# One-core hybrid attention layer: score bias and mask added on VectorE, gate units in another order, low halves on GpSimd

## The reference, cut to what matters

```python
mod = silu(c) @ w_ada + b_ada; shift, scale, gate = split(mod, 3)
h = rmsnorm(x, ln_gain) * (1 + scale) + shift
q_a, ckv, krope, g_a, q_b, k_b, v_b, q_i, k_i, w_i, g_b = split(h @ w_in)
# group A: latent attention, chunk-causal mask        -> o_a
# group B: an indexer scores keys, top-k keys per row are kept (k = 64 prompt, 36 sample), then
s = (q_b . k_sel) * 128**-0.5 + rel_bias[rel_bucket(sel - q_pos)]
s = where(valid, s, -inf);  o_b = softmax(s) @ v_sel
y = concat(rmsnorm(o_a, gain_a) * silu(g_a), rmsnorm(o_b, gain_b) * silu(g_b))
out = rmsnorm(x + gate * (y @ w_out), final_gain)
```

## Time and profile before

| what | value |
|---|---|
| time, 3 runs | median 1014.14 us (1013.35 to 1014.65) |
| profiled execution, own time | 1013.96 us |
| its span | 1012.2 us |
| TensorE busy | 941.5 us, 93% of the span, mean granted clock 0.986 |
| VectorE, ScalarE, GpSimd busy | 419.3, 341.0, 91.3 us |

### The profile page before, as it was taken

One profiled execution on the slowest core, in us unless ns is written; L12 is line 12 of the kernel. 1 busy time (PEld: TensorE's weight loads), 2 busy tenths in 40 slices (PEclk: granted clock), 3 DMA queues, 4 the chain that ended last, 5 costly groups with the idle time before them and its releaser, 6 DMA issues.

```text
span 1012.2 us, 14472 instructions
## 1 busy us (share of the span) xinstructions
PE 941.5 (93%) x5867; PEld 808.4 (80%) x5867; DVE 419.3 (41%) x865; ACT 341.0 (34%) x629; POOL 91.3 (9%) x165
## 2 busy tenths in 40 slices
PE   3798789999999999999999999999998899899996
PEld 0466577899998788888898998889986789688885
DVE  2222343436332244432324632349454346745562
ACT  2332342334212243323314522233333336433342
POOL 1000022102100000111102100010011001300000
PEclk9999899999999999999999999999999899899999
DMA  8999956665533224564426765345576536864423
GB/s 318 386 335 368 365 164 170 156 159 140 151 115 94 79 87 138 151 194 128 135 85 184 240 212 178 92 126 177 185 237 214 181 102 241 293 209 130 135 64 125
DMA packets 128403, 183.29 MB, mean 181 GB/s; under 512 B 29408, under 2 KB 79256, under 8 KB 127184
## 3 DMA queue, kind: packets, MB, share of 16 engines
q1 hardware_dynamic: 115744, 138.71, 44.1%
q0 software_dynamic: 12592, 43.65, 12.9%
HBM read 171.80 MB, written 10.52 MB: 180 GB/s over the span
## 4 chain that ended last, share of the span: by engine, by line
PE 84%; DMA 5%; ACT 3%; DVE 3%; issue 2%; SPq 2%; POOL 1%; DVEq 0%; ACTq 0%; POOLq 0%
PE proj L1697 31%; PE proj L1686 28%; PE proj L1713 2%; PE bankO L1670 2%; DMA araw<-in_w_ada 2%; SPq L696 2%; PE bankO L1794 1%; PE bankO L1803 1%; PE bankS L1713 1%; PE bankS L1686 1%; PE proj L1670 1%; PE bankS L1920 1%; PE bankT L1935 1%; DMA kload<-in_cache_dsa_k 1%; DMA raw<-in_w_in 1%
## 5 line engine op out<-in xcount | busy, mean ns | idle before, releaser
L1255 DVE TENSOR_TENSOR w_lo<-raw,w_hi 128x1024 fp32r<-128x1024 f32 (+2 forms) x164 | 193.6, 1185 | 233.2 <-ACT w_hi L919 232.8
L919 ACT ACTIVATE w_hi<-raw 128x1024 fp32r<-128x1024 f32 (+2 forms) x164 | 167.4, 1027 | 210.0 <-PE proj L1686 126.1
L1697 PE MATMUL proj<-hT_hi,w_hi 128*128 128x384 f32 x640 | 222.3, 347 | 1.1 <-ACT misc L919 1.1
L1697 PE MATMUL proj<-hT_hi,w_lo 128*128 128x384 f32 x640 | 214.8, 336 | 0.0
L1697 PE MATMUL proj<-hT_lo,w_hi 128*128 128x384 f32 x640 | 214.7, 335 | 0.0
L1686 PE MATMUL proj<-w_hi,hT_hi 128*128 128x512 f32 (+2 forms) x464 | 180.9, 390 | 16.1 <-DVE w_lo L1255 13.2
L1686 PE MATMUL proj<-w_lo,hT_hi 128*128 128x512 f32 (+2 forms) x464 | 176.6, 381 | 0.0
L1686 PE MATMUL proj<-w_hi,hT_lo 128*128 128x512 f32 (+2 forms) x464 | 176.5, 380 | 0.0
L1697 PEld LDWEIGHTS proj<-hT_hi,w_hi 128*128 128x128 f32 x640 | 120.7, 189 | 9.1 <-issue 7.0
L1697 PEld LDWEIGHTS proj<-hT_lo,w_hi 128*128 128x128 f32 x640 | 120.7, 189 | 0.7 <-issue 0.2
L1697 PEld LDWEIGHTS proj<-hT_hi,w_lo 128*128 128x128 f32 x640 | 120.5, 188 | 0.0
(11 more groups left out here) (346 smaller groups left out, 1033.3 us busy)
## 6 DMA issues: line engine op xcount, KB each, us to landing
raw<-in_w_in SPq DMA_DIRECT2D x104, 512.0 KB, 3.8
araw<-in_w_ada SPq DMA_DIRECT2D x128, 256.0 KB, 7.6
raw<-in_w_ada SPq DMA_DIRECT2D x32, 512.0 KB, 3.8
raw<-in_w_out SPq DMA_DIRECT2D x32, 512.0 KB, 3.9
raw<-in_w_in SPq DMA_DIRECT2D x32, 256.0 KB, 3.2
raw<-in_w_in SPq DMA_DIRECT2D x32, 128.0 KB, 2.5
wuk<-in_w_uk POOLq DMA_DIRECT2D x16, 256.0 KB, 3.7
kload<-in_cache_dsa_k POOLq DMA_DIRECT2D x8, 512.0 KB, 5.3
```

The lines of the kernel that those rows point to most:

```text
L919: return nc.scalar.activation(out, in_, func, scale=scale, **kw)
L1255: V.tensor_tensor(w_lo[:, SLOT[u], 0:w], raw_of(u)[:, 0:w], high(u)[:, 0:w].bitcast(F32), ALU.subtract).then_inc(lo_ready, 1)
L1697: ins = mm(banks[blk][:, 0:TOK], w[:, n, cols], a[:, kt, :], start=first and n == m == 0, stop=final and n == per - 1 and m == 2)
```

## The change

1. `units()` puts one `gate` unit behind each unit of `qi` and of `qb` (32 in all) and none elsewhere.
2. The matrices `rev` and `rep`, their loads and the matmuls with them are gone. The bias rows are written once to DRAM 128 times over (`skew_d`, 2 MB, from DRAM to DRAM at the place of the old bias read), so that a stride of one less than a row reads them in the order that the scores have. Prompt: VectorE adds mask and bias per head (`masked_bias`, for head h + 1 between the maximum and the wait for the exponential of head h). Sample: the mask goes to DRAM and comes back in eight DMAs into `comb` (`ld_mask`), VectorE adds the bias to it once (`comb`, 128 x 1152), and per sequence one operation adds `comb` to the scores and takes the maximum; a sign change follows, and ScalarE's exponential reads SBUF, where it read PSUM.
3. `yh`'s low half is on GpSimd, where it was on VectorE.
4. Group B's gate tiles have eight buffers of their own (`gl_b`); loads, `y`, `yh`, the load of `res`, of the layer's gate and of `final_gain` stand at other units.

```diff
     for n, u in enumerate(dense):
         out.append(u)
-        if n % 2 and len(gate) > TAIL:
+        if CHUNKS[u[0]][0] in ("qi", "qb"):
             out.append(gate.pop(0))
-    out += gate
...
+    put(u + 5, ("ld_mask", 0))
+    put(u + 7, ("comb", 0))
...
     for i in range(8):
         v = max(u + 2 + i // 2, LAST_UNIT["gb", i // 2] + (6 if i >= 6 else 2))
-        put(v - 2 - (i >= 6), ("ld_g", 8 + i))
+        put(max(u, v - 3), ("ld_g", 8 + i))
         put(v, ("y", 8 + i))
...
-        put(w0 + 1 + i // 2, ("yh", 8 + i))
-
-    put(w0, ("ld_gate", 0))
-    put(w0, ("ld_fgain", 0))
+        put(max(w0 + 1, v - 2 + (i >= 6)) + i // 2, ("yh", 8 + i))
+
+    put(max(w0, u + 1), ("ld_gate", 0), ("ld_fgain", 0))
...
-            load(rev[:], i["c_rev"].rearrange("p (a q) -> p a q", a=2), "const_in")
-            load(rep[:], i["c_rep"].rearrange("p (a q) -> p a q", a=DB), "const_in")
...
         def bias_rd(_):
             pool.wait_ge(sem("bias_out"), 16)
+            load(skew_d, bass.AP(bias_d.tensor, 0, [[NDELTA, HEADS], [0, P], [1, NDELTA]]), "skew_out")
+
+        def ld_skew(_):
+
+            pool.wait_ge(sem("skew_out"), 16)
             for h in range(HEADS):
                 load(hankel_s[DS * h:DS * (h + 1), :],
-                     bass.AP(bias_d.tensor, h * NDELTA + P - DS, [[1, DS], [1, NKEY]]), "hankel_s_in")
...
+        def ld_mask(_):
+
+            pool.wait_ge(sem("nsel_ready"), 1)
+            load(nsel_d, nsel[:, 2, 0:NKEY], "mask_out")
+            pool.wait_ge(sem("mask_out"), 16)
+            for h in range(HEADS):
+                load(comb[DS * h:DS * (h + 1), :, :],
+                     bass.AP(nsel_d.tensor, 0, [[NKEY, DS], [DS * NKEY, DB], [1, NKEY]]), "comb_in")
...
+        def yh(n):
+            src = o_aT if n < 8 else o_bT
+            pool.wait_ge(sem("hT_hi_ready"), KT + n + 1)
+            nc.gpsimd.tensor_tensor(hT_lo[:, n, :], src[:, n % 8, :], hT_hi[:, n, :].bitcast(F32),
+                                    ALU.subtract).then_inc(sem("hT_ready"), 1)
+
...
+        def masked_bias(h_):
+
+            if h_ < HEADS:
+                link(V.tensor_tensor(corner[:, h_ % 2, :], hankel[:, h_, P:SEQ], nsel[:, 0, 0:P], ALU.add))
+                link(V.tensor_tensor(hankel[:, h_, :], hankel[:, h_, :], nsel[:, 1, :], ALU.add))
+
...
+                dve.wait_ge(sem("nsel_ready"), NT)
+                dve.wait_ge(sem("hankel_in"), 16)
...
+            prompt_max("dp", h_, lambda p0, w: corner[:, h_ % 2, :] if p0 == 0 else hankel[:, h_, :], masked_bias)
+
+        def comb_(_):
+            dve.wait_ge(sem("comb_in"), 16 * HEADS)
+            dve.wait_ge(sem("hankel_s_in"), 16 * HEADS)
+            link(V.tensor_tensor(comb[:], comb[:], hankel_s[:].unsqueeze(1).broadcast_to([P, DB, NKEY]), ALU.add))
...
-        def yh(n):
-            src = o_aT if n < 8 else o_bT
-            dve.wait_ge(sem("hT_hi_ready"), KT + n + 1)
-            V.tensor_tensor(hT_lo[:, n, :], src[:, n % 8, :], hT_hi[:, n, :].bitcast(F32),
-                            ALU.subtract).then_inc(sem("hT_ready"), 1)
...
-                mm(out[:, c0:c0 + w], rev[:, 0, :], hankel[:, h_, SEQ - w:SEQ], start=True, stop=False)
-                ins = mm(out[:, c0:c0 + w], q_bT[:, h_, P * t:P * (t + 1)], kT[:, h_, 0:w], start=False, stop=True)
+                ins = mm(out[:, c0:c0 + w], q_bT[:, h_, P * t:P * (t + 1)], kT[:, h_, 0:w], start=True, stop=True)
...
-            for r in quads:
-                mm(out[r, 0:NKEY], rev[:, 1, r], hankel_s[:], start=True, stop=False)
-            for r in quads:
-                mm(out[r, 0:NKEY], rep[:, b, r], nsel[:, 2, 0:NKEY], start=False, stop=False)
             for m in range(2):
                 for g, r in enumerate(quads):
-                    ins = mm(out[r, 0:NKEY], qbd[:, 2 * g + m, :], kcT[:, 2 * g + m, :], start=False, stop=m == 1)
+                    ins = mm(out[r, 0:NKEY], qbd[:, 2 * g + m, :], kcT[:, 2 * g + m, :], start=m == 0, stop=m == 1)
```

More of the change, by code:

```diff
@@ L284, in plan @@
     run(u, "oa", 2)
-    put(u + 1, ("ld_kic", 0), ("wsel", 0))
+    put(u + 1, ("ld_kic", 0), ("wsel", 0), ("ld_skew", 0))
     u += 2
@@ L406, in constants @@
     negmask = np.concatenate([mask[:P, :P], mask[P:]], axis=1)
[L407 to L415, removed]
     diag = (np.arange(P)[:, None] % DS == np.arange(DS)).astype(np.float32)
@@ L419, in constants @@
     onehot[rel_bucket(np.minimum(delta, SEQ - 1)), np.arange(NDELTA)] = 1
-    return {"c_eye": eye, "c_cossin": cossin.reshape(P, -1), "c_negmask": negmask, "c_rev": rev.reshape(P, -1),
-            "c_rep": rep.reshape(P, -1), "c_diag": diag, "c_onehot": onehot}
+    return {"c_eye": eye, "c_cossin": cossin.reshape(P, -1), "c_negmask": negmask,
+            "c_diag": diag, "c_onehot": onehot}
 def build(nc, i, o):
@@ L449, in program @@
     eye = fixed("eye", [P, P])
-    rev = fixed("rev", [P, 2, P])
-    rep = fixed("rep", [P, DB, P])
+    comb = fixed("comb", [P, DB, NKEY])
     ones = fixed("ones", [P, P])
@@ L818, in ld_g @@
             stored(pool, "ga" if n < 8 else "gb", n // 2 % 4)
-            load(gl[:, n % GL, :], g_d[n], f"gl_in{n % GL}")
+            load(gate_slot(n)[0], g_d[n], gate_slot(n)[1])
         def ld_k(t):
@@ L831, in ld_hankel @@
             filled(pool, "ks", DB - 1)
-            load(hankel[:], bass.AP(bias_d.tensor, 0, [[1, P], [NDELTA, HEADS], [1, SEQ]]), "hankel_in")
+            load(hankel[:], bass.AP(skew_d.tensor, P - 1, [[NDELTA - 1, P], [P * NDELTA, HEADS], [1, SEQ]]), "hankel_in")
         def ld_v(_):
@@ L1137, in y @@
         def y(n):
-            act.wait_ge(sem(f"gl_in{n % GL}"), 16 * (n // GL + 1))
-            nc.scalar.activation(gl[:, n % GL, :], gl[:, n % GL, :], ACT.Silu).then_inc(sem("gl_silu"), 1)
+            slot, loaded, count = gate_slot(n)
+            act.wait_ge(sem(loaded), count)
+            nc.scalar.activation(slot, slot, ACT.Silu).then_inc(sem("gl_silu"), 1)
         def yh(n):
@@ L1362, in kn, with prompt_max @@
             V.tensor_copy(knT[:, h_, :], bank["O"][:, 0:SEQ]).then_inc(free["O"], 1)
-        def prompt_max(kind, h_, mask):
+        def prompt_max(kind, h_, mask, between=None):
             filled(dve, kind, h_, "S")
@@ L1373, in prompt_max @@
                             ALU.mult).then_inc(sem(kind + "_max"), 1)
+            if between:
+                between(h_ + 1)
             dve.wait_ge(sem(kind + "_exp"), h_ + 1)
@@ L1419, in sample_max @@
             e = b % 2
-            V.tensor_reduce(stat[:, 32 + 2 * e:33 + 2 * e], bank["S"][:, 0:NKEY], AX.X, ALU.max,
-                            negate=True).then_inc(sem(kind + "_max"), 1)
-            dve.wait_ge(free["S"], USES[kind, b, "S"] + 1)
+            if kind == "ss":
+                V.tensor_reduce(stat[:, 32 + 2 * e:33 + 2 * e], bank["S"][:, 0:NKEY], AX.X, ALU.max,
+                                negate=True).then_inc(sem("ss_max"), 1)
+                dve.wait_ge(free["S"], USES["ss", b, "S"] + 1)
+            else:
+                V.tensor_tensor_reduce(probs[:, e, 0:NKEY], bank["S"][:, 0:NKEY], comb[:, b, :], 1.0, -BIG, ALU.add,
+                                       ALU.max, stat[:, 40 + 2 * e:41 + 2 * e]).then_inc(free["S"], 1)
+                dve.wait_ge(free["S"], USES["ds", b, "S"] + 1)
+                V.tensor_scalar(stat[:, 32 + 2 * e:33 + 2 * e], stat[:, 40 + 2 * e:41 + 2 * e], -1.0, None,
+                                ALU.mult).then_inc(sem("ds_max"), 1)
+                dve.wait_ge(sem("ds_exp"), b + 1)
             link(V.reciprocal(stat[:, 44 + 2 * e:45 + 2 * e], stat[:, 36 + 2 * e:37 + 2 * e]))
@@ L1564, in _ @@
                  "kn": kn, "mp": mp, "dp": dp, "mv": mv, "dv": dv, "ql": ql, "krc": krc_, "st": st, "ss": ss, "ds": ds,
-                 "so": so, "oa": oa, "osq": osq_, "ysq": ysq, "y": y, "yh": yh, "wsel": wsel_, "kic": kic_, "ip": ip,
+                 "so": so, "oa": oa, "osq": osq_, "ysq": ysq, "y": y, "wsel": wsel_, "kic": kic_, "ip": ip,
                  "iacc": iacc,
-                 "tk": tk, "kl": kl, "ks": ks, "dsoT": dsoT}
+                 "tk": tk, "comb": comb_, "kl": kl, "ks": ks, "dsoT": dsoT}
         link(V.memset(stat[:], 0.0))
```

35 lines of the change are left out of this document (21 added, 14 removed).

## The result

The changed kernel took 1003.88 us (median of 4 runs, 1003.2 to 1008.2) against 1013.99 for the kernel before on the same chip: a ratio of 0.991, 95% interval 0.989 to 0.993. It is faster by 10 us. Forecast were 27, and the range of 978 to 997 did not hold the time. The profiled execution is the one of 1008.2 us, so its parts are compared by stretches and not by its end.

The account below looks back on a forecast made before the run. TensorE, busy 93% of the span, was taken as the bound. From 1013.96 us, gains of 9.3, 9.7, 1.7, 5.0, 6.0, 1.9 less losses of 3.3, 2.1, 0.9, 0.5 gave 987.2 us; range 978 to 997 (0.83).

Parts of the forecast that it names:

- Matmuls removed: Attention steps: reversing and replicating products go, 5.2 us in prompt and 4.1 in sample steps, a gain of 9.3.
- Waits in the attention steps: Group B's attention steps: whole units as cover remove 10.7 us of waits, less 1.0 for late `vc`, gain 9.7.
- L1878: Group A's sample steps: two waits of 0.9 us go as the first `gate` unit moves past them, gain 1.7.
- start of `wo`: First `wo` unit: the late `w_lo` wait goes, as `y` and three `gate` units leave that place, gain 5.0 us.
- `wuv`: GpSimd's load queue: without the `rev` and `rep` loads ahead, TensorE's wait for the `wuv` load goes, gain 1.9 us.
- Clock: Two late clock dips, 3.4 us lost in each window: both go with whole units throughout, gain 6.0 us.
- First past keys: Second `kload`, behind the store of the second `gate` half: it lands late, loss 2.1 us (0 to 4.7).
- The tail: Late `wo` units: `gl` 14 and 15 load last behind 6 MB, needed by `wo 0 7`, loss 0.5 us (0 to 5).
- Top-k: Top-k stretch: VectorE's chain of 33.6 us against TensorE's 30.4, TensorE loses 3.3 us (0 to 6).
- the reciprocal's: Reciprocal in `ysq`: a unit's split stands behind it on VectorE, 6.7 us against 5.8 of cover, loss 0.9.
- `yh` at nothing: Sixteen low-half subtractions on GpSimd: no cost unless one takes over 4 us; VectorE's lighter load only helps.
- only the matmuls are saved: Rival, whole kernel: waits move with the `gate` units to other places, only 9.3 us gained, 1004.7 us; chance 0.06.

Follow-up runs that it names:

- experiments 5 and 6: Two parts tried alone on the kernel before: bias and mask only, 1008.9 us (0.995); new unit order only (b_order), 1013.0 us (0.999).
- b_order: Kernel before with only the new unit order, the `gl_b` tiles and the new places of loads: 1013.0 us (0.999).
- a_three: Changed kernel with second past keys loaded ahead of the store, all `gl_b` loads ahead of the 6 MB burst, VectorE's top-k work spread: 989.5, later 992.2 us.
- a_four: a_three with VectorE's top-k rounds spread from the second on, `kl` 1 and 2 and `comb` later still: 987.7 us (0.974).
- a_three_again: a_three unchanged, timed once more in a later group of runs on the same chip as a_four: 992.2 us.

## Why the prediction was wrong

**Matmuls removed, 9.3: right**, with the order of units in place (experiments 5 and 6: 8 to 9 between b_order and after, `yh` included). By themselves they were worth 4.8.

**Waits in the attention steps, 9.7 net; L1878, 1.7; start of `wo`, 5.0; `wuv`, 1.9: right in the main.** The waits are gone from the rows but for the one of 1.0 for `kcT`, of which 0.7 is left, and the "issue" rows at `dso`, where a late `vc` (charged with 1.0) would show, hold 0.5 to 1.6. Two of the terms were read from one profile and are smaller in the other: `wuv` is 1.9 in one and 0.9 in the other, `kload` 2.1 and nothing. The copy inside DRAM, put under 10 us, took 13.8 from issue to landing, and nothing waits behind it.

**Clock, 6.0: the step that failed most.** It said that with whole units throughout both dips are gone. They are gone from where they were, but the clock fell at the two new long waits, 6.8 and 3.4 us at half the rate, 0.9 of them within a wait: 4.7 us come back of 6.0. The step went by the whole units that replace short ones, and not by the waits that the same forecast put in. Without those waits (a_three, a_four) no dip is left between the first 130 us and the last 10; a_three_again had two of 3.4 us in the top-k stretch (last section).

**First past keys, 2.1: the mechanism was right and the size too small**, 4.0, and 0.7 ahead of it for `kcT`: the upper bound. From the end of the `gate` unit (742.8) the store began not 0.5 later, as put, but 3.1. VectorE's sum stood behind a split that had waited 8.68 for ScalarE's `w_hi`:

```profile
744.08 1.23 DVE L1276 TENSOR_TENSOR w_lo<-raw,w_hi 128x1024 fp32r<-128x1024 f32 x1 [8.68 <-ACT w_hi L938]
745.23 0.42 DVE L1632 TENSOR_TENSOR modA<-proj,modA 128x256 f32<-128x256 f32 x1
```

The issues (2.0) and the landing (5.3) were as put.

**The tail, 0.5: wrong in its place and size**, 4.8 at the end of its bounds (0 to 5). The estimate of the landing was 31 us after `wo 0 2` starts and it was 34 (901.5 for 867.4). And it asked when `wo 0 7` needs `gl` 14, while ScalarE's queue makes `wo 0 6` need it, one unit of 4.1 us earlier: the copies of `hT_hi` 12 and 13 stand behind the wait for 14. That is 4.3 too little, the second largest failure, and 1.7 of the clock's 4.7 stand behind it.

**Top-k, 3.3: near.** 3.7 of waits, at the places named (the second `kl`, `qb 2 0`, `qb 2 1`; the third, of 0.75, at `qi 1 1` is the reciprocal's, forecast 0.9). Not in the sum were 1.8 more: between two `gate` units a whole unit takes 4.39 from start to start, before, the two that stood in a row took 4.30 and 4.26; over 16 units that is the rest. Why is not shown.

**`yh` at nothing: wrong by 1.4** (`dt7`), and the reason given ("VectorE loses as much work, which only helps") is refuted. The rule of the Trainium skill that was weighed against it ("GPSIMD Engine Reference", section 1: shared SBUF interfaces, contention when VectorE reads two SBUF inputs) is what the traces show, 1.22 against 1.66 on the mean and up to 2.09 us for a split. Its section 3.1 gives a ratio of 1.96 for a two-input add; here it was 1.02 to 0.55, 1.85, for one of 384. Whether the 6 us of its section 2.1 for a first call are paid, no run shows: the first subtraction took 1.03 and began 0.1 us behind the copy it waited for, but GpSimd had stood idle for 17 us ahead of it, which would hide them:

```profile
848.35 2.00 POOL L877 TENSOR_TENSOR hT_lo<-o_aT,hT_hi 128x384 fp32r<-128x384 f32 x2 [17.09 <-ACT hT_hi L938]
```

Over all, what the change takes away was forecast right in the main. What it adds was put at 6.8 us of stalls and was 13.9 in the same four places (3.7, 4.7, 0.75 and 4.8), with 4.7 of clock behind them, 1.8 at unit changes and 1.4 of contention: 15.0 over the sum, where the balance has 15. With only the places of some loads and steps mended the kernel comes to 989.5 and 992.2 (a_three) and 987.7 (a_four), for the 987.2 forecast. That these lie so near is luck in part: in the four places a_three has 2.7 of stalls for the 6.8 put, 4.1 less, and the 1.8 and the 1.4, which the sum left out, make up for 3.2 of it.

Of the rivals, the one with 1004.7 ("only the matmuls are saved", chance 0.06) is nearest to the measured 1003.9, and experiment 6 bears out its gist: the order alone gained nothing. But the waits did not go with the `gate` units; new ones arose at other places.

## What to carry to other kernels

A change of order moves waits: list for each load its place in its queue, and what stands ahead of it in bytes as well as in issues, and move the short loads with a near deadline ahead of the burst; here two such moves and a wider spread of one engine's work were worth 12 to 16 us by medians, more than the change itself. Look at what stands behind a waiting instruction on an in-order engine, since its deadline is that of its successor. And charge each long wait of TensorE twice: for itself, and for the clock behind it (here 3.0 us for the wait of 4.0 and 1.7 for the one of 4.8); several fixes on one path are to be tried together, since a later wait for a transfer swallows what the earlier fix gained.
